# Gates and branch outputs of a decoder layer computed with tokens as the stationary operand

## The chip, the core and the metric

The kernel runs on one core of one Trainium2 chip. The metric is the device time of one execution in microseconds (us). TensorE (PE in the profile) multiplies: a stationary operand of 128x128 is loaded (LDWEIGHTS, the row PEld), a moving operand streams through it, and the products are summed in PSUM. VectorE (DVE), ScalarE (ACT) and GpSimd (POOL) do the rest, and SyncE (SP) issues nearly all DMAs.

## The reference

One layer, 256 tokens, 2048 features, all in float32. Three branches (convolution A, gated linear attention B, block attention C) work on the same normalised input `h`. The part that is changed is the merge of the branches:

```python
y_a = conformer_conv_branch(...)      # ends in  a @ w_conv_out[i]   (512 -> 2048)
y_b = gla_branch(...)                 # ends in  o @ w_gla_out[i]    (512 -> 2048)
y_c = moba_branch(...)                # ends in  o @ w_moba_out[i]   (1024 -> 2048)
gates = jax.nn.sigmoid(h @ w_gate[i] + b_gate[i]).reshape(b_sz, s, N_BRANCH, d)
merged = gates[:, :, 0] * y_a + gates[:, :, 1] * y_b + gates[:, :, 2] * y_c
x = x + merged @ w_out[i]
```

After it come a gated MLP with a short causal convolution and a gated input embedding, which the change leaves alone.

## The kernel before, in words

**Chunks.** Every weight matrix is read once, in chunks of 256 rows x 512 columns (512 KB). A chunk `c` goes through a ring of four buffers: SP loads it into `raw` (L323) once DVE has split the chunk four before it (`chunk_split`); ACT casts it to `w_hi` (`high`, L801), once PE has used chunk `c`-4 (`chunk_used`); DVE computes `w_lo = raw - w_hi` (`split`, L1084); PE multiplies. Each product is made of three matmuls, high by high, high by low and low by high, in the type fp32r.

**Two shapes of a chunk on PE.** `feature_chunk` (L457) holds a 128x128 block of the weights stationary and moves the 256 tokens of the activations: 2 x 4 blocks x 3 products = 24 matmuls of 256 columns. The result has features on partitions, as `[P, 4, 256]`. `token_chunk` (L481) holds 128 tokens x 128 features of the activations stationary and moves 512 weight columns: 2 halves of the tokens x 2 x 3 = 12 matmuls of 512 columns. The result has tokens on partitions, as `[P, 2, 512]`. Both fill the same two PSUM banks of an accumulator (`acc[0]` or `acc[1]`, by turns).

**Groups.** The program is a fixed list of 254 chunks, then loops for the MLP. A group of chunks makes 512 output columns. Around the change the list reads `mv` (chunks 74 to 89, two groups of 8), `yA` (90 to 97, four groups of 2), `gA` (98 to 129, four groups of 8), `yB` (130 to 137), `gB` (138 to 169), `yC` (170 to 185, four groups of 4), `gC` (186 to 217), `wout` (218 to 249, four groups of 8), `ple` (250 to 253). `y` are the branches' output projections, `g` the gates. `mv`, `wout` and `ple` use the token shape, the `y` and `g` groups the feature shape: 32 + 96 = 128 chunks. `LAST[name, g]` is the last chunk of a group.

**Order on the engines.** No scheduler is at work: each engine has a written program over `c`, and what hangs on a chunk number stands behind that chunk's own step. ACT's and DVE's steps for chunk `c` run when PE is some three chunks behind, because the cast of `c` waits until PE has used `c`-4. What an engine does beside its chunks is put at offsets: for the group `gC, g`, ACT computes `gt = tanh(0.5 a + 0.5 bias)` in four instructions (L905, one per 128 features, since the bias is one number per partition) behind the cast of `LAST`+4; DVE multiplies `yb = (gt + 1) yb` (L1389) and adds `full = merged + yb` (L1395) behind the split of `LAST`+5; ACT casts `full` to `m_hi` (L805) and DVE makes `m_lo` (L1090), which `wout` uses as the stationary operand, 128 tokens of 128 features. For `gA` and `gB` the multiplication stands at `LAST`+6. ACT copies the `y` groups out of PSUM (L850).

**Other work between the chunks.** In `yA` and `gA` PE also does the last levels of the linear attention (`gla_level`, behind chunks 91, 95, 99, 103, 107, each waiting for DVE's `level_ready`), its outputs and norms (112, 117, 119). From `yB` to the middle of `gB` it does eight attention heads, three small pieces each (`scores`, `turn_probs`, `probs_v`). Behind chunk 190 it turns `p`. In `wout` `turn_x` (L607) transposes 128x128 blocks of `x`, eight matmuls at a time. That makes 33 such pieces in chunks 90 to 217.

Of the kernel before, what the change touches and what calls it, by code (L numbers as in the profile page):

```python
# [37 lines left out]
P = 128  # L38
# [78 lines left out]
R_MIX, R_CB, R_LG, R_LB, R_GLA, R_Q, R_K, R_BG, R_FFN, R_PLE, R_ALL = 0, 16, 20, 24, 28, 29, 30, 31, 79, 95, 111  # L117
# [8 lines left out]
def trunk(nc, x, p, norm_mix_g, w_in, conv_w, conv_b, conv_ln_g, conv_ln_b, w_conv_out,  # L126
# [36 lines left out]
    small = new("small", [P, 16])  # L163
    arena = (top[0] + KB - 1) // KB * KB
# [17 lines left out]
    merged = ar("merged", [P, KD, S], 0)  # L182
    yb = ar("yb", [P, KD, S], 16)
# [15 lines left out]
    gt = ar("gt", [P, QD, S], 86)  # L199
# [62 lines left out]
    gate_ready, gate_merged = sem("gate_ready"), sem("gate_merged")  # L262
    p_turned = sem("p_turned")
# [30 lines left out]
    def wait_taken(eng, n):  # L294
# [12 lines left out]
            (gla_norm_g[0], R_GLA), (moba_q_norm_g[0], R_Q), (moba_k_norm_g[0], R_K), (b_gate[0], R_BG),  # L307
# [8 lines left out]
    def _(sp):  # L316
# [15 lines left out]
        for name, g, c0, n in GROUPS:  # L332
            if name == "gB" and g == 1:
                sp.wait_ge(chunk_used, FIRST["gB", 0])
                sp.dma_start(ptok[:], p[0, 0].rearrange("(t p) n -> p t n", p=P)).then_inc(p_landed, 16)
            for j in range(n):
# [113 lines left out]
    def _(pe):  # L450
# [166 lines left out]

        for c in range(UP1):
# [10 lines left out]
            if name in ("val", "gate", "qk", "gr", "mq", "mk", "mq2", "mk2", "gA", "gB", "gC"):  # L629
# [3 lines left out]
            elif name in ("gv", "mv"):  # L633
# [9 lines left out]
            elif name == "yA":  # L643
                pe.wait_ge(unit_split, U_A + 1)
                feature_chunk(c, s, a_hi, a_lo, 2 * j, first, last)
            elif name == "yB":
                pe.wait_ge(unit_split, U_B + 1)
                feature_chunk(c, s, o_hi, o_lo, 2 * j, first, last)
            elif name == "yC":
                pe.wait_ge(unit_split, U_C + 2 * j + 2)  # L650
                feature_chunk(c, s, c_hi, c_lo, 2 * j, first, last)
# [77 lines left out]
            for q in range(4):  # L729
                if c == LAST["wout", q] + 1:  # L730
                    turn_x(q, NUMBER["wout", q], U_X1 + q - 1 if q >= 2 else None)
# [49 lines left out]
    def _(act):  # L781
# [63 lines left out]

        def take(number, dst, src, scale=None):
# [5 lines left out]
        for c in range(START, UP1 + 12):  # L852
# [4 lines left out]
            if e in GROUP_AT and e == LAST[GROUP_AT[e][:2]] and not (GROUP_AT[e][0] == "ple" and e == c - RING):  # L857
# [30 lines left out]
                elif name == "yA":  # L888
                    take(number, merged[:, 4 * g:4 * g + 4, :], a[:], 0.5)
                elif name in ("yB", "yC"):  # L890
# [4 lines left out]
                    take(number, yb[:, 4 * g:4 * g + 4, :], a[:], 0.5)  # L895
                elif name in ("gA", "gB", "gC"):
                    b = "ABC".index(name[1])

                    if b == 2 and g:
                        act.wait_ge(unit_full, U_M + g)  # L900
                    elif 4 * b + g:
                        act.wait_ge(gate_merged, 4 * b + g)
                    for j in range(QD):
                        col = R_BG + 16 * b + 4 * g + j
# [658 lines left out]
```

## Time and profile before

| | |
|---|---|
| median of 3 runs | 1628.25 us (1627.68 to 1631.37) |
| the profiled execution | 1627.26 us, of which the span is 1625.3 us |
| granted TensorE clock, mean over the span | 0.998 of full speed |
| PE busy | 1609.0 us (99%) |
| DVE busy | 1031.2 us (63%) |
| ACT busy | 779.5 us (48%) |
| DMA | 294.30 MB, mean 181 GB/s |

The span is the time between the first and the last instruction; 2 us of the execution lie around it. Matmuls are pipelined, so a PE busy of 99% only says that there are no long holes; how fast it goes is read from the distance between the starts of its matmuls. A timeline row gives the start in us from the span's start, the duration in us, the engine, the line, the operation, the tiles written and read, and behind them in brackets how long the engine was idle before and what ended that.

### The profile page before, as it was taken

What the parts mean: (1) busy time and instruction counts of PE and PEld (TensorE: products, weight loads), DVE (VectorE), ACT (ScalarE), POOL (GpSimd) and SP (SyncE); (2) the same over time, 40 slices, a digit from 0 to 9 for tenths busy, and PEclk for the clock granted to TensorE, in tenths of its full rate; (3) what the DMA queues carried; (4) which work ended last, traced back from release to release, by engine and by line L of the source; (5) the groups of instructions that cost most, each with busy time, mean ns of one, the idle gap of its engine ahead of it and who ended that gap; (6) DMA issues with size and microseconds to landing.
All of it is one profiled execution on the core that took longest, in us unless ns stands there. A gap on an engine that the chain in (4) does not pass through costs nothing.

```text
span 1625.3 us, 26115 instructions
## 1 busy us (share of the span) xinstructions
PE 1609.0 (99%) x10146; PEld 1459.3 (90%) x10146; DVE 1031.2 (63%) x1203; ACT 779.5 (48%) x935; POOL 32.3 (2%) x53
## 2 busy tenths in 40 slices
PE   7999999999999999999999999999999999999998
PEld 7989998999999999988788888888888888888887
DVE  6598655664557545555467777765447777765554
ACT  5444444444455544455455555543335455554443
POOL 5000000000000000000000000000000000000000
PEclk9999999999999999999999999999999999999999
DMA  7666555555555565555566665655565666556564
GB/s 232 181 178 181 159 166 156 156 167 155 178 169 157 171 191 181 178 189 186 175 181 193 186 188 182 186 199 194 193 191 174 194 194 193 184 185 194 175 202 148
DMA packets 154275, 294.30 MB, mean 181 GB/s; under 512 B 9383, under 2 KB 11795, under 8 KB 154192
## 3 DMA queue, kind: packets, MB, share of 16 engines
q1 hardware_dynamic: 153648, 292.85, 58.6%
q8 instruction: 60, 0.98, 0.2%
q0 software_dynamic: 512, 0.27, 0.1%
q14 instruction: 23, 0.19, 0.0%
q10 hardware_dynamic: 32, 0.01, 0.0%
HBM read 291.00 MB, written 2.10 MB: 180 GB/s over the span
## 4 chain that ended last, share of the span: by engine, by line
PE 98%; DVE 1%; DMA 0%; ACT 0%; issue 0%; POOL 0%; SPq 0%; ACTq 0%; DVEq 0%
PE psum L474 20%; PE psum L453 12%; PE psum L454 11%; PE psum L455 11%; PE psum L477 10%; PE psum L490 10%; PE psum L491 10%; PE psum L492 10%; PE psum L570 1%; PE psum L507 1%; DMA xtok<-in_x 0%; PE psum L615 0%; PE psum L524 0%; PE psum L584 0%; PE psum L603 0%; PE psum L593 0%
## 5 line engine op out<-in xcount | busy, mean ns | idle before, releaser
L1084 DVE TENSOR_TENSOR w_lo<-raw,w_hi 128x1024 fp32r<-128x1024 f32 x550 | 670.1, 1223 | 518.1 <-ACT w_hi L801 517.8
L801 ACT CAST w_hi<-raw 128x1024 fp32r<-128x1024 f32 x550 | 574.8, 1049 | 666.8 <-PE psum L455 290.7
L453 PE MATMUL psum<-h_both,w_hi 128*128 128x256 f32 x1296 | 371.1, 286 | 3.0 <-DVE h_both L1090 3.0
L455 PE MATMUL psum<-h_both,w_lo 128*128 128x256 f32 x1296 | 367.6, 284 | 0.0
L454 PE MATMUL psum<-h_both,w_hi 128*128 128x256 f32 x1296 | 367.6, 284 | 0.0
L474 PE MATMUL psum<-h_both,w_hi 128*128 128x512 f32 x1408 | 352.6, 392 | 0.0
L474 PEld LDWEIGHTS psum<-h_both,w_hi 128*128 128x128 f32 x1408 | 253.3, 189 | 45.3
L453 PEld LDWEIGHTS psum<-h_both,w_hi 128*128 128x128 f32 x1296 | 249.6, 193 | 3.6 <-issue 3.2
L454 PEld LDWEIGHTS psum<-h_both,w_hi 128*128 128x128 f32 x1296 | 249.7, 193 | 0.1
L455 PEld LDWEIGHTS psum<-h_both,w_lo 128*128 128x128 f32 x1296 | 249.5, 192 | 0.0
L477 PEld LDWEIGHTS psum<-h_both,w_lo 128*128 128x128 f32 x1408 | 192.1, 190 | 13.7
L477 PE MATMUL psum<-h_both,w_lo 128*128 128x256 f32 x1408 | 196.3, 282 | 0.0
L490 PE MATMUL psum<-w_hi,f_hi 128*128 128x512 f32 x352 | 137.2, 390 | 0.0
L492 PE MATMUL psum<-w_hi,f_lo 128*128 128x512 f32 x352 | 137.0, 389 | 0.0
L491 PE MATMUL psum<-w_lo,f_hi 128*128 128x512 f32 x352 | 137.0, 389 | 0.0
L490 PE MATMUL psum<-w_hi,h_both 128*128 128x512 f32 x224 | 87.8, 392 | 0.0
L491 PE MATMUL psum<-w_lo,h_both 128*128 128x512 f32 x224 | 87.2, 389 | 0.0
L492 PE MATMUL psum<-w_hi,h_both 128*128 128x512 f32 x224 | 87.2, 389 | 0.0
L492 PEld LDWEIGHTS psum<-w_hi,f_lo 128*128 128x128 f32 x352 | 66.1, 188 | 13.8
L490 PEld LDWEIGHTS psum<-w_hi,f_hi 128*128 128x128 f32 x352 | 66.1, 188 | 13.6
L491 PEld LDWEIGHTS psum<-w_lo,f_hi 128*128 128x128 f32 x352 | 66.1, 188 | 13.4
L1169 DVE SCALAR_TENSOR_TENSOR val<-apad,cw,val 128x256 f32<-128x256 f32 x120 | 50.2, 480 | 1.1
(248 smaller groups left out, 1466.7 us busy)
## 6 DMA issues: line engine op xcount, KB each, us to landing
raw<-in_w_up SPq DMA_DIRECT2D x176, 512.0 KB, 3.8
raw<-in_w_gate SPq DMA_DIRECT2D x96, 512.0 KB, 3.7
raw<-in_w_in SPq DMA_DIRECT2D x90, 512.0 KB, 3.6
raw<-in_w_down SPq DMA_DIRECT2D x88, 512.0 KB, 4.5
raw<-in_w_out SPq DMA_DIRECT2D x32, 512.0 KB, 4.4
raw<-in_w_ple_gate SPq DMA_DIRECT2D x32, 512.0 KB, 4.5
raw<-in_w_moba_out SPq DMA_DIRECT2D x16, 512.0 KB, 3.7
raw<-in_w_conv_out SPq DMA_DIRECT2D x8, 512.0 KB, 3.7
```

The source lines that it names most:

```text
L453: nc.tensor.matmul(dst, stat_hi, mov_hi, start=first, stop=False, skip_group_check=True)
L454: nc.tensor.matmul(dst, stat_hi, mov_lo, start=False, stop=False, skip_group_check=True)
L455: return nc.tensor.matmul(dst, stat_lo, mov_hi, start=False, stop=last, skip_group_check=True)
L474: nc.tensor.matmul(wide[part][:, j, :], w_hi[:, c % RING, w], h_both[:, kt + k, :, :].rearrange("p h s -> p (h s)"), start=first and k == ...
L477: mm = nc.tensor.matmul(wide[part][:, j, S:2 * S], w_lo[:, c % RING, w], h_hi[:, kt + k, :], start=False, stop=last and k == 1, skip_group ...
L490: nc.tensor.matmul(o, sh, w_hi[:, c % RING, w], start=first and k == 0, stop=False, skip_group_check=True)
L491: nc.tensor.matmul(o, sh, w_lo[:, c % RING, w], start=False, stop=False, skip_group_check=True)
L492: mm = nc.tensor.matmul(o, sl, w_hi[:, c % RING, w], start=False, stop=last and k == 1, skip_group_check=True)
L507: mm = nc.tensor.matmul(dst[:, 2 * j + t:2 * j + t + 1], src[:, j, t * P:(t + 1) * P], ones[:, 0:1], start=True, stop=True, skip_group_che ...
L801: A.copy(w_hi[:, c % RING, :], raw[:, c % RING, :]).then_inc(chunk_high, 1)
L1084: V.tensor_tensor(w_lo[:, c % RING, :], raw[:, c % RING, :], w_hi[:, c % RING, :].bitcast(F32), ALU.subtract).then_inc(chunk_split, 1)
L1169: last = V.scalar_tensor_tensor(val[:, j, :], src, w, val[:, j, :], ALU.mult, ALU.add)
```

## The change

The `y` and `g` groups use the token shape. Their results, `merged`, `yb` and `gt` lie with tokens on partitions. Since the gate's bias then differs along the row, it is no longer a number per partition: SP loads 512 of its values ahead of each `g` group, repeated on all 128 partitions (256 KB in SBUF, twelve times), DVE adds it to the sums out of PSUM (`gate_sum`, behind the split of `LAST`+3), and ACT computes one `tanh` of 128x1024 in place. The multiplication of `gC` moves to `LAST`+4. The merged result has tokens on partitions, while `wout` needs features there, so PE turns it by eight transposes per group (`turn_m`, behind chunk `LAST`+2 of `gC`), and ACT and DVE make `m_hi` and `m_lo` out of PSUM (`m_high` at `LAST`+6, `m_low` at `LAST`+7). ACT's waits on `gate_merged` ahead of the gates are gone. The rows of the bias leave the small parameters' table, which falls from 111 rows to 63.

```diff
     rows = [(norm_mix_g[0], R_MIX), (conv_b[0], R_CB), (conv_ln_g[0], R_LG), (conv_ln_b[0], R_LB),
-            (gla_norm_g[0], R_GLA), (moba_q_norm_g[0], R_Q), (moba_k_norm_g[0], R_K), (b_gate[0], R_BG),
+            (gla_norm_g[0], R_GLA), (moba_q_norm_g[0], R_Q), (moba_k_norm_g[0], R_K),
             (norm_ffn_g[0], R_FFN), (norm_ple_g[0], R_PLE)]
...
                 sp.dma_start(ptok[:], p[0, 0].rearrange("(t p) n -> p t n", p=P)).then_inc(p_landed, 16)
+            if name in ("gA", "gB", "gC"):
+                k = 4 * "ABC".index(name[1]) + g
+                if k >= 2:
+                    wait_taken(sp, NUMBER["g" + "ABC"[(k - 2) // 4], (k - 2) % 4])
+                sp.dma_start(bias[:, k % 2, :], b_gate[0, k * W:(k + 1) * W].unsqueeze(0).broadcast_to([P, W])).then_inc(bias_landed[k % 2], 16)
             for j in range(n):
...
 
+        def turn_m(g):
+
+            pe.wait_ge(unit_full, U_M + g + 1)
+            if g >= 2:
+                pe.wait_ge(unit_split, U_M + g - 1)
+            src = tokens(full[:, (U_M + g) % 2, :, :])
+            for j in range(QD):
+                for t in range(TT):
+                    mm = nc.tensor.transpose(turned(g)[:, j, t * P:(t + 1) * P], src[:, t, j * P:(j + 1) * P], ident[:])
+            mm.then_inc(m_turned, 1)
+
         for c in range(UP1):
...
             first, last = j == 0, j == n - 1
-            if name in ("val", "gate", "qk", "gr", "mq", "mk", "mq2", "mk2", "gA", "gB", "gC"):
+            if name in ("val", "gate", "qk", "gr", "mq", "mk", "mq2", "mk2"):
                 if c < START:
                     pe.wait_ge(unit_split, U_H + c + 1)
                 feature_chunk(c, s, h_hi, h_lo, 2 * j, first, last)
-            elif name in ("gv", "mv"):
+            elif name in ("gv", "mv", "gA", "gB", "gC"):
                 token_chunk(c, s, h_hi, h_lo, 2 * j, first, last)
...
                 pe.wait_ge(unit_split, U_A + 1)
-                feature_chunk(c, s, a_hi, a_lo, 2 * j, first, last)
+                token_chunk(c, s, a_hi, a_lo, 2 * j, first, last)
             elif name == "yB":
                 pe.wait_ge(unit_split, U_B + 1)
-                feature_chunk(c, s, o_hi, o_lo, 2 * j, first, last)
+                token_chunk(c, s, o_hi, o_lo, 2 * j, first, last)
             elif name == "yC":
                 pe.wait_ge(unit_split, U_C + 2 * j + 2)
-                feature_chunk(c, s, c_hi, c_lo, 2 * j, first, last)
+                token_chunk(c, s, c_hi, c_lo, 2 * j, first, last)
             elif name == "wout":
...
             for q in range(4):
+                if c == LAST["gC", q] + 2:
+                    turn_m(q)
                 if c == LAST["wout", q] + 1:
...
 
+        def m_high(g):
+
+            act.wait_ge(m_turned, g + 1)
+            A.copy(m_hi[:, QD * g:QD * g + QD, :], turned(g)).then_inc(unit_high, 1)
+
         def take(number, dst, src, scale=None):
...
                 elif name == "yA":
-                    take(number, merged[:, 4 * g:4 * g + 4, :], a[:], 0.5)
+                    take(number, merged[:, :, g * W:(g + 1) * W], tokens(a), 0.5)
                 elif name in ("yB", "yC"):
                     if name == "yB" and g == 0:
                         act.wait_ge(att_ready, 1)
                     if name == "yC":
                         act.wait_ge(gate_merged, 4 + g + 1)
-                    take(number, yb[:, 4 * g:4 * g + 4, :], a[:], 0.5)
+                    take(number, yb[:, :, g * W:(g + 1) * W], tokens(a), 0.5)
                 elif name in ("gA", "gB", "gC"):
-                    b = "ABC".index(name[1])
-
-                    if b == 2 and g:
-                        act.wait_ge(unit_full, U_M + g)
-                    elif 4 * b + g:
-                        act.wait_ge(gate_merged, 4 * b + g)
-                    for j in range(QD):
-                        col = R_BG + 16 * b + 4 * g + j
-                        last = A.activation(gt[:, j, :], a[:, j, :], ACT.Tanh, bias=parh[:, col:col + 1], scale=0.5)
-                    last.then_inc(taken[number % 2], 1)
+                    wait_taken(act, number)
+                    A.activation(gt[:], gt[:], ACT.Tanh, scale=0.5).then_inc(gate_ready, 1)
                 elif name == "ple":
...
             for g in range(4):
-                if c == LAST["gC", g] + 5:
+                if c == LAST["gC", g] + 6:
                     earlier()
-                    unit(U_M + g)
+                    m_high(g)
                 if c == LAST["wout", g] + 4:
...
 
+        def gate_sum(k, last_chunk, number):
+
+            dve.wait_ge(chunk_used, last_chunk + 1)
+            dve.wait_ge(bias_landed[k % 2], 16 * (k // 2 + 1))
+            V.tensor_tensor(gt[:], tokens(acc[number % 2]), bias[:, k % 2, :].unsqueeze(1).broadcast_to([P, TT, W]),
+                            ALU.add).then_inc(taken[number % 2], 1)
+
+        def m_low(g):
+
+            dve.wait_ge(unit_high, U_M + g + 1)
+            m = slice(QD * g, QD * g + QD)
+            V.tensor_tensor(m_lo[:, m, :], turned(g), m_hi[:, m, :].bitcast(F32), ALU.subtract).then_inc(unit_split, 1)
+
         def x_mean(n):
...
                     name = "g" + "ABC"[b]
-                    q = slice(4 * g, 4 * g + 4)
-                    if c == LAST[name, g] + (6 if b < 2 else 5):
+                    q = slice(g * W, (g + 1) * W)
+                    if c == LAST[name, g] + 3:
                         earlier()
-                        wait_taken(dve, NUMBER[name, g])
+                        gate_sum(4 * b + g, LAST[name, g], NUMBER[name, g])
+                    if c == LAST[name, g] + (6 if b < 2 else 4):
+                        earlier()
+                        dve.wait_ge(gate_ready, 4 * b + g + 1)
+                        wait_taken(dve, NUMBER["y" + "ABC"[b], g])
                         if b == 0:
-                            wait_taken(dve, NUMBER["yA", g])
-                            V.scalar_tensor_tensor(merged[:, q, :], gt[:], 1.0, merged[:, q, :], ALU.add, ALU.mult).then_inc(gate_merged, 1)
+                            V.scalar_tensor_tensor(merged[:, :, q], gt[:], 1.0, merged[:, :, q], ALU.add, ALU.mult).then_inc(gate_merged, 1)
                         else:
-                            wait_taken(dve, NUMBER["yB" if b == 1 else "yC", g])
-                            step(V.scalar_tensor_tensor(yb[:, q, :], gt[:], 1.0, yb[:, q, :], ALU.add, ALU.mult))
+                            step(V.scalar_tensor_tensor(yb[:, :, q], gt[:], 1.0, yb[:, :, q], ALU.add, ALU.mult))
                             sync()
                             if b == 1:
-                                V.tensor_tensor(merged[:, q, :], merged[:, q, :], yb[:, q, :], ALU.add).then_inc(gate_merged, 1)
+                                V.tensor_tensor(merged[:, :, q], merged[:, :, q], yb[:, :, q], ALU.add).then_inc(gate_merged, 1)
                             else:
 
-                                V.tensor_tensor(full[:, (U_M + g) % 2, :, :], merged[:, q, :], yb[:, q, :], ALU.add).then_inc(unit_full, 1)
-                    if b == 2 and c == LAST[name, g] + 6:
+                                V.tensor_tensor(tokens(full[:, (U_M + g) % 2, :, :]), merged[:, :, q], yb[:, :, q],
+                                                ALU.add).then_inc(unit_full, 1)
+                    if b == 2 and c == LAST[name, g] + 7:
                         earlier()
-                        unit(U_M + g)
+                        m_low(g)
             if c == FIRST["gC", 0] + 8:
```

How the order moves is shown at two places, both in the gates of branch C. First PE, from the end of the last chunk but one ahead of the turn into the chunk behind it, with the change (`w_hi` and `w_lo` are the chunk's halves, `h_both` the normalised input, `full` the merged group, `ident` the unit matrix):

```order
L498 MATMUL psum<-w_hi,h_both 128x512
L499 MATMUL psum<-w_lo,h_both 128x512
L500 MATMUL psum<-w_hi,h_both 128x512
L634 MATMUL psum<-ident,full 128x128 x8
L498 MATMUL psum<-w_hi,h_both 128x512
L499 MATMUL psum<-w_lo,h_both 128x512
```

The same place before, where nothing stands between the chunks:

```order
L453 MATMUL psum<-h_both,w_hi 128x256
L454 MATMUL psum<-h_both,w_hi 128x256
L455 MATMUL psum<-h_both,w_lo 128x256
L453 MATMUL psum<-h_both,w_hi 128x256
L454 MATMUL psum<-h_both,w_hi 128x256
```

The matmuls are half as many and twice as wide, and eight transposes stand between two chunks.

Then DVE, in the group `gC, 0` and up to the next group's gate; before (`p_lo` is the low part of the embedding input, which has its place here too):

```order
L1402 COPY full<-psum 128x512
L1084 TENSOR_TENSOR w_lo<-raw,w_hi 128x1024 x2
L1090 TENSOR_TENSOR p_lo<-full,p_hi 128x512
L1084 TENSOR_TENSOR w_lo<-raw,w_hi 128x1024 x2
L1389 SCALAR_TENSOR_TENSOR yb<-gt,yb 128x1024
L1395 TENSOR_TENSOR full<-merged,yb 128x1024
L1084 TENSOR_TENSOR w_lo<-raw,w_hi 128x1024
L1090 TENSOR_TENSOR m_lo<-full,m_hi 128x1024
L1084 TENSOR_TENSOR w_lo<-raw,w_hi 128x1024 x7
```

and with the change (`bias` is the repeated bias):

```order
L1436 COPY full<-psum 128x512
L1102 TENSOR_TENSOR w_lo<-raw,w_hi 128x1024 x2
L1169 TENSOR_TENSOR gt<-psum,bias 128x1024
L1108 TENSOR_TENSOR p_lo<-full,p_hi 128x512
L1102 TENSOR_TENSOR w_lo<-raw,w_hi 128x1024
L1422 SCALAR_TENSOR_TENSOR yb<-gt,yb 128x2x512
L1428 TENSOR_TENSOR full<-merged,yb 128x1024
L1102 TENSOR_TENSOR w_lo<-raw,w_hi 128x1024 x3
L1176 TENSOR_TENSOR m_lo<-psum,m_hi 128x1024
L1102 TENSOR_TENSOR w_lo<-raw,w_hi 128x1024 x4
```

The addition of the bias is new, the multiplication stands one split earlier, and `m_lo` two splits further behind the merge.

## Rows read from the trace of the kernel before

**Rows 1.** The page: busy times, and the chain that ended last.
```profile
PE 1609.0 (99%) x10146; PEld 1459.3 (90%) x10146; DVE 1031.2 (63%) x1203; ACT 779.5 (48%) x935; POOL 32.3 (2%) x53
...
PE 98%; DVE 1%; DMA 0%; ACT 0%; issue 0%; POOL 0%; SPq 0%; ACTq 0%; DVEq 0%
```

**Rows 2.** Waits of PE: what for, us in total, times, longest.
```profile
PE psum L534 <- DMA pst<-in_norm_mix_g: 3.9, 1, 3.9
PE psum L524 <- POOL ms L396: 3.1, 2, 2.3
PE psum L453 <- DVE h_both L1090: 3.0, 1, 3.0
PE psum L544 <- DMA xtok<-in_x: 1.0, 1, 1.0
```

**Rows 3.** Windows: length, busy time and count by engine, clock, DMA.
```profile
624.58:647.62 23.04, 23.04 (x195) 23.04 (x193) 13.70 (x12) 10.80 (x13) 0.00 (x0) 1.00 0.58 183
427.00:555.00 128.00, 128.00 (x1049) 127.11 (x1048) 79.43 (x119) 68.72 (x108) 0.00 (x0) 1.00 0.55 167
248.23:259.11 10.88, 10.88 (x49) 9.01 (x48) 4.85 (x7) 5.23 (x6) 0.00 (x0) 1.00 0.68 190
```

**Rows 4.** Timeline of PE in `wout`: a turn of `x` between token matmuls.
```profile
717.98 0.39 PE L492 MATMUL psum<-w_hi,m_lo 128*128 128x512 f32 x1
718.21 1.03 PE L615 MATMUL psum<-ident,xtok 128*128 128x128 f32 x8
719.00 0.48 PE L490 MATMUL psum<-w_hi,m_hi 128*128 128x512 f32 x1
719.32 0.40 PE L491 MATMUL psum<-w_lo,m_hi 128*128 128x512 f32 x1
```

**Rows 5.** Timeline of PE in `gA`: sixteen small matmuls between feature matmuls.
```profile
396.21 0.28 PE L455 MATMUL psum<-h_both,w_lo 128*128 128x256 f32 x1
396.33 1.95 PE L524 MATMUL psum<-ident,ms 128*128 128x128 f32 x16
398.03 0.36 PE L453 MATMUL psum<-h_both,w_hi 128*128 128x256 f32 x1
...
398.59 0.28 PE L454 MATMUL psum<-h_both,w_hi 128*128 128x256 f32 x1
```

**Rows 6.** Timeline of PE in `mv`: the same sixteen between token matmuls.
```profile
270.49 0.39 PE L492 MATMUL psum<-w_hi,h_both 128*128 128x512 f32 x1
...
272.41 0.48 PE L490 MATMUL psum<-w_hi,h_both 128*128 128x512 f32 x1
...
273.43 0.39 PE L491 MATMUL psum<-w_lo,h_both 128*128 128x512 f32 x1
```

**Rows 7.** Timeline of ACT at the end of the group `gC, 1` (chunk 201).
```profile
647.87 1.05 ACT L801 CAST w_hi<-raw 128x1024 fp32r<-128x1024 f32 x1 [1.83 <-PE psum L455]
648.95 1.57 ACT L905 ACTIVATE gt<-psum,parh 128x256 f32<-128x256 f32 x4
650.75 1.05 ACT L801 CAST w_hi<-raw 128x1024 fp32r<-128x1024 f32 x1 [0.23 <-PE psum L455]
```

**Rows 8.** Groups by shape, chunks 90 to 217: busy, mean ns, idle before.
```profile
L1389 DVE SCALAR_TENSOR_TENSOR yb<-gt,yb 128x1024 f32<-128x1024 f32 x7 | 8.6, 1225 | 0.2
L850 ACT ACTIVATE yb<-psum 128x1024 f32<-128x1024 f32 x8 | 8.2, 1025 | 0.3
...
L1342 DVE TENSOR_TENSOR full<-gr,psum 128x1024 f32<-128x1024 f32 x1 | 1.2, 1223 | 0.0
...
L1090 DVE TENSOR_TENSOR p_lo<-full,p_hi 128x512 fp32r<-128x512 f32 x1 | 0.7, 691 | 0.0
```

**Rows 9.** Timeline of DVE: the merge of `gC, 1`.
```profile
654.35 1.23 DVE L1395 TENSOR_TENSOR full<-merged,yb 128x1024 f32<-128x1024 f32 x1
```

**Rows 10.** Timeline of DVE: what the last attention level waits for.
```profile
355.21 0.68 DVE L1206 TENSOR_TENSOR lqk<-gqk,ex 128x512 f32<-128x512 f32 x1
```

**Rows 11.** Timeline of PE: that level, behind chunk 107.
```profile
356.63 0.72 PE L573 MATMUL psum<-lqk 64*128 64x128 f32 x8
```

**Rows 12.** Timeline of SP: the load of chunk 206 is the first of these.
```profile
641.56 20.14 SPq L323 DMA_DIRECT2D raw<-in_w_gate  x7
```

**Rows 13.** DMA issues by line: KB each, median us to landing.
```profile
raw<-in_w_gate SPq DMA_DIRECT2D x96, 512.0 KB, 3.7
...
ptok<-in_p SPq DMA_DIRECT2D x1, 256.0 KB, 4.3
```

More of the change, by code:

```diff
@@ L114 @@
 U_X2 = U_F + PAIRS1 + PAIRS2
-R_MIX, R_CB, R_LG, R_LB, R_GLA, R_Q, R_K, R_BG, R_FFN, R_PLE, R_ALL = 0, 16, 20, 24, 28, 29, 30, 31, 79, 95, 111
+R_MIX, R_CB, R_LG, R_LB, R_GLA, R_Q, R_K, R_FFN, R_PLE, R_ALL = 0, 16, 20, 24, 28, 29, 30, 31, 47, 63
 START = 8
@@ L163, in trunk @@
     small = new("small", [P, 16])
+    bias = new("bias", [P, 2, W])
     arena = (top[0] + KB - 1) // KB * KB
@@ L181, in trunk @@
     masks = ar("masks", [P, 7, P // 2], 28)
-    merged = ar("merged", [P, KD, S], 0)
-    yb = ar("yb", [P, KD, S], 16)
+    merged = ar("merged", [P, TT, D], 0)
+    yb = ar("yb", [P, TT, D], 16)
     mq = ar("mq", [P, HEADS, S], 32)
@@ L198, in trunk @@
     tmpg = ar("tmpg", [P, QD * S], 82)
-    gt = ar("gt", [P, QD, S], 86)
+    gt = ar("gt", [P, TT, W], 86)
     o_hi = ar("o_hi", [P, QD, S], 68, F32R)
@@ L262, in trunk @@
     gate_ready, gate_merged = sem("gate_ready"), sem("gate_merged")
+    bias_landed = [sem("bias_landed0"), sem("bias_landed1")]
+    m_turned = sem("m_turned")
     p_turned = sem("p_turned")
```

## The prediction

> **What bounds the kernel now.** I read the page's busy times and the chain that ended last first [rows 1]: PE is busy for 99% of the span, and 98% of the last chain lies on PE. Such a share says nothing of how fast PE goes, so the list of PE's waits came next [rows 2]. It has four rows, 11.0 us together, and all of them belong to the start, before or at the first chunks. From then on PE waits for nobody: neither for a split, nor for the attention pieces, nor for a load. So the time of the stage that is changed is the distance between the starts of PE's matmuls, and only what changes that distance, or makes PE wait, moves the end.
>
> The windows give the distance for both shapes [rows 3]. The group `gC, 1` is 8 feature chunks of 24 matmuls, 192 in 23.04 us: 0.120 us each and 2.88 us a chunk. (The count 195 holds three more that reach over the window's edges.) Four token chunks in `mv`, 48 matmuls, take 10.88 us: 0.2267 us each and 2.72 us a chunk. The granted clock is 1.00 in both. The token shape moves the same columns in half as many instructions, and it is 0.16 us a chunk faster, on the same input `h` as the gates use.
>
> **What the shape gives.** 128 chunks (32 of `y`, 96 of `g`) x 0.16 us = 20.5 us, all of it on PE and therefore on the path.
>
> Here the Trainium skill speaks against the change. Its page "TensorE: Matmul & The Clock Gate", section "Back-to-back issue gap", gives an isolated matmul 262 cycles for 256 columns and 518 for 512, almost the columns alone. By that, 24 narrow matmuls and 12 wide ones would differ by 72 cycles or 0.03 us, and the 128 chunks would give 3.8 us. The trace disagrees with it for a stream of weight load and matmul: 0.120 us and 0.2267 us are both above its 0.109 and 0.216 us, and the narrow one by more in proportion.
>
> **What PE gets in addition.** (a) Four turns of the merged result, eight 128x128 transposes each. `wout` shows such a turn between token chunks [rows 4]: from 717.98 to 719.32 us lie two steps between the chunks' own matmuls, which take 0.45 us undisturbed, so the turn costs 0.89 us. Four cost 3.6 us. (b) The 33 small pieces between chunks 90 and 217 now stand beside token chunks. The same sixteen small matmuls cost 2.38 - 5 x 0.12 = 1.78 us between feature matmuls [rows 5] and 2.94 - 5 x 0.2267 = 1.81 us between token matmuls [rows 6]. 33 x 0.03 = 1.0 us; I keep 0 and 1.5 us as its ends, since only one kind of piece is seen in both surroundings.
>
> **Waits that could come.** Let T be the moment at which PE starts the chunk behind a gate's group; for `gC, 1` it is 647.62 us [rows 3]. The cast that waits for the same semaphore starts at T+0.25 [rows 7]. The new addition of the bias can start there too; it is an elementwise operation of 128x1024 with one operand in PSUM, 1.22 us [rows 8] (L1342), and ends at T+1.5. The tanh in one instruction I price as ACT's 128x1024 out of PSUM, 1.03 us [rows 8] (L850); it ends at T+2.55. DVE's split of `LAST`+4 goes from T+1.5 to T+2.7, the multiplication to T+3.95, the addition to T+5.2 (1.225 us each [rows 8, 9]). PE comes to the turn two chunks on, at T+5.44, but fetches the weights of a matmul one step earlier, so it looks at about T+5.2. That is a tie: 0 to 0.3 us of waiting, and I take 0.1 us for three of the turns. In the first group DVE also has the low part of the embedding input in between, 0.69 us [rows 8] (L1090): the merge is ready at T+5.9, and I take 0.6 us. Together 0.9 us. As the other end I take the moment at which the merge is ready today, 655.58 us or T+7.96 [rows 9]: if the earlier place in the order gained nothing, each turn would wait 2.5 us, 10 us in all.
>
> The chain of the attention levels has the least air of the other waits. For the last level DVE ends at 355.21 + 0.68 = 355.89 us [rows 10], and PE starts it at 356.63 [rows 11]. DVE's part hangs on the end of chunk 105, and the three chunks from there to the level get 3 x 0.16 = 0.48 us shorter, so 0.26 us of 0.74 are left, less PE's look ahead. The new bias addition of `gA, 0` stands in that very stretch of DVE, but DVE is idle there while ACT makes the exponentials. I take 0.1 us, between 0 and 0.5.
>
> **What lies beside.** The bias additions, 12 x 1.22 = 14.7 us of DVE, cost nothing in themselves: DVE is busy 13.70 of 23.04 us in `gC, 1` and 79.43 of 128 us in the densest stretch of attention heads [rows 3], with 14.9 of 22.7 us and some 84 of 123 us afterwards. Behind each addition stand a split and the merge, and PE needs that split three chunks later. ACT loses four small tanh (1.57 us, [rows 7]) for one of 1.03 us, and its cast no longer stands behind a wait for the merge. `m_high` and `m_low` are as long as the instructions that they replace; the last of them is done by about T+12 us, and `wout` asks for it at its seventh chunk, T+17. Where that cover went, PE would wait for the difference once. The one bias DMA of POOL that goes is at the start, off the path.
>
> The twelve repeated loads stand in SP's queue ahead of a group's first chunk, and everything behind them waits for them. SP's own wait ahead of them is for an addition eight chunks or more ago, done by then. How much they may take: the load of chunk 206 is issued at 641.56 us [rows 12], lands 3.7 us later [rows 13], and its cast starts at 650.75 [rows 7], a margin of 5.5 us, and of 4.8 us with four chunks 0.16 us shorter. A plain load of the same 256 KB lands in 4.3 us [rows 13], and it shares the engines rather than holding them. I take 0, with the case below as the other end.
>
> **The sum.** 20.5 - 3.6 - 1.0 - 0.9 - 0.1 = 14.9 us. The profiled execution takes 1627.26 us, so 1612.4 us; the median of the runs is 1.0 us above the profiled one, and I predict 1613.4 us. With nothing waiting and the pieces no dearer the gain is 16.9 us; with every turn waiting 2.5 us it is 5 to 6 us.
>
> **Rivals.**
> 1. *The turns wait as long as the merge takes today.* Each link of addition, tanh, split, multiplication and addition passes a semaphore, and the tie at T+5.2 bears no extra. Full price 4 x 2.6 = 10.4 us in place of 0.9, gain 5.4, time 1622.9 us. Against it: the merge moves forward by a whole split, and each link's duration is known. Chance 0.13, with most of that for a part of the price.
> 2. *The levels and heads come late.* PE's time between two of them shrinks by 0.16 us a chunk and DVE has the additions in between. Eight heads at 0.5 us are 4 us: 1617.4 us. For it speaks the 0.26 us of the last level; against it that no head shows a wait now [rows 2]. Chance 0.05.
> 3. *Only columns count.* Then the shape gives nothing, and the turns, pieces and waits remain, 5.6 us: 1633.9 us. With the 3.8 us it is 1630.1 us, no measurable change (that part of the case is the skill's rule on the issue gap). Four chunks at 2.72 us against eight at 2.88 us [rows 3] speak plainly against it. Chance 0.02.
> 4. *Slower: the repeated load holds the queue.* All 128 partitions read the same 2 KB. If such a transfer were confined to one of the 16 DMA engines, it would go at 183 / 0.58 / 16 = 20 GB/s [rows 3] and take 13 us; the chunk behind it would be 8.5 us late, twelve times 102 us, time about 1715 us. It decides from 4.8 + 14.9 / 12 = 6.0 us per load on; above that the kernel is slower than before. The only 256 KB load in the trace, 4.3 us, is below, but repeats nothing. Chance 0.03.
>
> **How the numbers follow.** The forecast has 0.77. Its own spread is 1611 to 1616 us. The range, 1610.8 to 1618 us, takes in the case with no waits and dearer or cheaper pieces, the second rival and the small part of the first; outside lie its full price and the last two. A measurement of this kernel tells about 0.2% or 3.3 us from no change. The forecast and the first two rivals are faster, 0.95; the third, near no change, 0.02; the fourth slower, 0.03.
>
> **What the profile of the changed kernel would show.** A group of `gC` between turns in 21.8 us, 0.227 us from matmul to matmul; four transposes of `full` by eight, the first with a wait for DVE of about half a microsecond, the others with none or 0.1 us; no other new wait of PE; bias loads that land in 3 to 5 us; the stages behind `ple` as long as before and some 15 us earlier. I would be wrong if a token chunk in the `y` or `g` groups took more than 2.75 us, if the turns showed waits of 1 us and more each, or if casts of ACT stood waiting for `raw`.

## The result, and the profile after

| | before | changed |
|---|---|---|
| median | 1627.97 us (1626.97 to 1631.37, 4 runs) | 1613.89 us (1611.17 to 1614.10, 4 runs) |
| profiled execution, span | 1627.26 us, 1625.3 us | 1614.08 us, 1612.0 us |

The ratio is 0.9906 with a 95% interval of 0.9888 to 0.9924: the change takes 14.1 us off, where 14.9 us and a time of 1613.4 us were predicted. A later set of runs of both kernels gave 1611.92 us against 1628.60 us, 16.7 us off.

The page of the changed kernel, answering to [rows 1]:

```profile
PE 1596.1 (99%) x8642; PEld 1383.0 (86%) x8642; DVE 1044.7 (65%) x1215; ACT 774.5 (48%) x899; POOL 32.3 (2%) x52
...
PE 97%; DVE 1%; DMA 1%; ACT 1%; issue 0%; POOL 0%; SPq 0%; DVEq 0%; ACTq 0%
```

PE has 1504 matmuls fewer (128 chunks x 12, less 4 x 8 transposes) and is still the bound. Its waits, answering to [rows 2]:

```profile
PE psum L542 <- DMA pst<-in_norm_mix_g: 4.3, 1, 4.3
PE psum L461 <- DVE h_both L1108: 3.0, 1, 3.0
PE psum L532 <- POOL ms L404: 2.3, 1, 2.3
PE psum L552 <- DMA xtok<-in_x: 0.7, 1, 0.7
PE psum L498 <- DVE w_lo L1102: 0.4, 1, 0.4
PE psum L634 <- DVE full L1428: 0.2, 1, 0.2
```

Four are old. One of these, `ms` L404, is 2.3 us long and stands between `ple` and the MLP, in both kernels; it matters below. Of the two new waits, L634 is the first turn. L498 is at the very end, where DVE's split stands in its queue behind a wait for an output DMA to land; nothing of the change is near it.

Windows of the changed kernel, with the columns of [rows 3]: eight chunks of `yC`, and the stretch around the start of the MLP.

```profile
565.10:586.86 21.76, 21.76 (x98) 18.02 (x97) 9.81 (x8) 10.44 (x10) 0.00 (x0) 1.00 0.65 211
778.00:800.00 22.00, 19.74 (x101) 16.83 (x100) 10.46 (x16) 9.34 (x10) 1.60 (x1) 0.92 0.54 161
```

The first shows 96 matmuls in 21.76 us, 2.72 us a chunk, as read from `mv` ahead of the change. The DMAs now bring 211 GB/s and nobody waits for them. The second has a granted clock of 0.92, of which more below.

The trace can be cut at the first matmul of every chunk, since the order on PE is fixed. The next table gives the time between such starts in us for each stage; it was worked out from the two traces and is no view of the profile:

| stretch | before | changed | difference |
|---|---|---|---|
| up to the first chunk | 16.43 | 15.43 | -1.00 |
| chunks 0 to 89 (unchanged groups) | 281.39 | 282.03 | +0.64 |
| `yA` | 26.47 | 25.31 | -1.16 |
| `gA` | 102.61 | 97.77 | -4.84 |
| `yB` | 25.23 | 24.06 | -1.17 |
| `gB` | 102.90 | 98.74 | -4.16 |
| `yC` | 46.08 | 43.52 | -2.56 |
| `gC` (three turns) | 92.59 | 90.65 | -1.94 |
| `wout` (one turn), `ple` | 98.87 | 99.68 | +0.81 |
| from the last `ple` chunk to the end | 832.70 | 834.83 | +2.13 |

From `yA` to `ple` the sum is -15.0 us: 20.5 us from the shape, less 4.0 us for the turns and 1.5 us for the 33 small pieces. The last line is no part of the change: 1.5 us is a lower clock at the start of the MLP, and 0.6 us lies at the very end, around the wait for the output's DMA. In the first two lines PE starts 1.0 us earlier, but more of the low clock at the start (6.8 us long in both traces) then falls into chunks 0 and 1, which gives 0.4 us back (together -0.6 us); 0.25 us more is spent at chunk 10.

The turn in `gC`, in the timeline of PE of the changed kernel:

```profile
637.39 0.39 PE L500 MATMUL psum<-w_hi,h_both 128*128 128x512 f32 x1
637.62 1.03 PE L634 MATMUL psum<-ident,full 128*128 128x128 f32 x8
638.41 0.48 PE L498 MATMUL psum<-w_hi,h_both 128*128 128x512 f32 x1
638.72 0.39 PE L499 MATMUL psum<-w_lo,h_both 128*128 128x512 f32 x1
```

Read as [rows 4]: 638.72 - 637.39 - 2 x 0.2267 = 0.88 us, and no wait in brackets. DVE's side of it, with T = 632.18 us:

```profile
632.43 1.22 DVE L1169 TENSOR_TENSOR gt<-psum,bias 128x1024 f32<-128x1024 f32 x1 [0.41 <-PE psum L500]
633.57 1.22 DVE L1102 TENSOR_TENSOR w_lo<-raw,w_hi 128x1024 fp32r<-128x1024 f32 x1
634.90 1.23 DVE L1422 SCALAR_TENSOR_TENSOR yb<-gt,yb 128x1024 f32<-128x1024 f32 x1
636.16 1.23 DVE L1428 TENSOR_TENSOR full<-merged,yb 128x1024 f32<-128x1024 f32 x1
```

The merge ends at 637.39 us, T+5.21, and PE starts the first weight load of the turn at 637.44 us, T+5.26. The tie that the prediction saw is there, and it comes out with nothing lost. The first group has `p_lo` in between, and there the turn waits:

```profile
614.32 0.39 PE L500 MATMUL psum<-w_hi,h_both 128*128 128x512 f32 x1
614.89 1.09 PE L634 MATMUL psum<-ident,full 128*128 128x128 f32 x8 [0.18 <-DVE full L1428]
615.74 0.48 PE L498 MATMUL psum<-w_hi,h_both 128*128 128x512 f32 x1
```

The bracket says 0.18 us, but the start is 0.57 us behind the last chunk matmul in place of 0.23. The weight load waits for the merge too: here it starts at 614.89 us, together with its matmul, where in the other turn it started 0.18 us ahead of it. The wait costs 0.4 us in chunk starts (3.91 us for this chunk against 3.51 us for the three others).

### The profile page after: what moved, and what is told of

It is laid out like the page before. It is cut to its first block, busy times and chain, and to the rows that moved or that the text cites. A ratio compares the mean times of both kernels' runs of the same rounds, so it can differ in the third digit from the quotient of the medians.

```text
span 1612.0 us, 23109 instructions
## 1 busy us (share of the span) xinstructions
PE 1596.1 (99%) x8642; PEld 1383.0 (86%) x8642; DVE 1044.7 (65%) x1215; ACT 774.5 (48%) x899; POOL 32.3 (2%) x52
## 4 chain that ended last, share of the span: by engine, by line
PE 97%; DVE 1%; DMA 1%; ACT 1%; issue 0%; POOL 0%; SPq 0%; DVEq 0%; ACTq 0%
PE psum L482 20%; PE psum L498 17%; PE psum L500 17%; PE psum L499 17%; PE psum L485 10%; PE psum L461 4%; PE psum L462 4%; PE psum L463 4%; PE psum L578 1%; PE psum L515 1%; PE psum L623 0%; PE psum L532 0%; DMA out<-fin 0%; DVE w_lo L1102 0%; ACT junk L839 0%; DMA xtok<-in_x 0%
## 5 line engine op out<-in xcount | busy, mean ns | idle before, releaser
L482 PEld LDWEIGHTS psum<-h_both,w_hi 128*128 128x128 f32 x1408 | 254.2, 190 | 45.6
L498 PE MATMUL psum<-w_hi,h_both 128*128 128x512 f32 x608 | 240.5, 396 | 0.4 <-DVE w_lo L1102 0.4
L500 PE MATMUL psum<-w_hi,h_both 128*128 128x512 f32 x608 | 236.9, 390 | 0.0
L499 PE MATMUL psum<-w_lo,h_both 128*128 128x512 f32 x608 | 236.8, 389 | 0.0
L485 PEld LDWEIGHTS psum<-h_both,w_lo 128*128 128x128 f32 x1408 | 192.1, 190 | 13.7
L485 PE MATMUL psum<-h_both,w_lo 128*128 128x256 f32 x1408 | 196.3, 282 | 0.0
L461 PE MATMUL psum<-h_both,w_hi 128*128 128x256 f32 x528 | 151.6, 287 | 3.0 <-DVE h_both L1108 3.0
L462 PE MATMUL psum<-h_both,w_hi 128*128 128x256 f32 x528 | 150.5, 285 | 0.0
L463 PE MATMUL psum<-h_both,w_lo 128*128 128x256 f32 x528 | 150.5, 285 | 0.0
L498 PE MATMUL psum<-w_hi,f_hi 128*128 128x512 f32 x352 | 137.2, 390 | 0.0
L500 PEld LDWEIGHTS psum<-w_hi,h_both 128*128 128x128 f32 x608 | 114.1, 188 | 24.4
L498 PEld LDWEIGHTS psum<-w_hi,h_both 128*128 128x128 f32 x608 | 114.2, 188 | 24.1 <-DVE w_lo L1102 0.8
L499 PEld LDWEIGHTS psum<-w_lo,h_both 128*128 128x128 f32 x608 | 114.3, 188 | 22.5
L461 PEld LDWEIGHTS psum<-h_both,w_hi 128*128 128x128 f32 x528 | 102.5, 194 | 3.4 <-issue 3.2
L462 PEld LDWEIGHTS psum<-h_both,w_hi 128*128 128x128 f32 x528 | 102.6, 194 | 0.1
L463 PEld LDWEIGHTS psum<-h_both,w_lo 128*128 128x128 f32 x528 | 102.5, 194 | 0.0
```

The lines of the kernel that those rows point to most:

```text
L461: nc.tensor.matmul(dst, stat_hi, mov_hi, start=first, stop=False, skip_group_check=True)
L462: nc.tensor.matmul(dst, stat_hi, mov_lo, start=False, stop=False, skip_group_check=True)
L463: return nc.tensor.matmul(dst, stat_lo, mov_hi, start=False, stop=last, skip_group_check=True)
L482: nc.tensor.matmul(wide[part][:, j, :], w_hi[:, c % RING, w], h_both[:, kt + k, :, :].rearrange("p h s -> p (h s)"), start=first and k == ...
L485: mm = nc.tensor.matmul(wide[part][:, j, S:2 * S], w_lo[:, c % RING, w], h_hi[:, kt + k, :], start=False, stop=last and k == 1, skip_group ...
L498: nc.tensor.matmul(o, sh, w_hi[:, c % RING, w], start=first and k == 0, stop=False, skip_group_check=True)
```

## The experiments

**Two narrow matmuls in place of a wide one.** In the gate chunks, same operands, same layout, same everything around:

```diff
-nc.tensor.matmul(o, sh, w_hi[:, c % RING, w], ...)          # 512 columns, three products
+parts = 2 if narrow else 1                                   # narrow: gA, gB, gC
+n_ = W // parts
+for q_ in range(parts):
+    o = dst[:, t * W + q_ * n_:t * W + (q_ + 1) * n_]
+    w = slice(k * W + q_ * n_, k * W + (q_ + 1) * n_)
+    nc.tensor.matmul(o, sh, w_hi[:, c % RING, w], ...)       # and the two other products
```

> The changed kernel, but in the 96 gate chunks each product of 512 columns is issued as two of 256 with the same stationary operand, so a chunk is again 24 matmuls of 256 columns while layout, bias, tanh and turns stay as changed. Theory: the gain is a fixed cost per matmul, 0.2267 us = 512/2.4 GHz + 13 ns and 0.120 us = 256/2.4 GHz + 13 ns, so 12 matmuls less are 0.16 us. Expected 0.120 us from start to start and 2.88 us a chunk in the gates, 96 x 0.16 = 15.4 us longer than the changed kernel, about 1629 us. Rival: the gain comes from what is stationary (128 tokens of h against weight blocks that were just written, or the repeat of the same stationary operand); then a chunk stays near 2.72 us and the time near 1614 us.

Measured 1628.63 us (10 runs), 0.9994 of the kernel before (0.9984 to 1.0004). `gA` takes 102.60 us and `gB` 102.90 us, to a hundredth what they took before the change. Four of its gate chunks in a window:

```profile
409.20:420.72 11.52, 11.52 (x98) 11.52 (x97) 6.12 (x5) 4.19 (x4) 0.00 (x0) 1.00 0.57 183
```

96 matmuls in 11.52 us, 0.120 us each. The rival falls: neither what is held stationary nor the layout matters, only into how many instructions the columns are cut. Bias loads, added bias and new tanh are all still there, so the run also shows that they cost the stages `gA` and `gB` nothing.

**Four of 128 columns.** The same with `parts = 4`.

> As the previous one, with four pieces of 128 columns: 48 matmuls a gate chunk. If the cost is columns/2.4 GHz + 13 ns at every width, one takes 0.067 us and a chunk 3.2 us, the kernel 96 x 0.48 = 46 us above the changed one, about 1660 us. Rival: below some width the weight load between two matmuls sets the pace (the small attention matmuls of 64 columns start 0.10 us apart); then a matmul takes about 0.10 us, a chunk 4.8 us, and the kernel is some 200 us above, about 1814 us.

Measured 1920.19 us (one run). Two windows of it, the first at a granted clock of 1.00, the second at 0.50:

```profile
528.02:549.46 21.44, 21.44 (x194) 21.44 (x194) 6.13 (x5) 4.19 (x4) 0.00 (x0) 1.00 0.32 100
380.00:440.00 60.00, 60.00 (x285) 59.66 (x284) 10.33 (x10) 6.28 (x6) 0.00 (x0) 0.50 0.19 57
```

At 2.4 GHz, 192 matmuls take 21.44 us, 0.112 us each: hardly less than one of 256 columns. So columns/2.4 GHz + 13 ns (0.120 - 0.107 and 0.2267 - 0.2133 us) holds for 256 and 512 columns and not for 128, where a pair of weight load and matmul takes 0.112 us in place of 0.067. That is the rival's case. Its 48 x 0.112 = 5.36 us a chunk give 253 us, and the kernel is 306 us above the changed one; the rest is the second row. PE was issuing without a hole, and the clock stood at 1.2 GHz for 95.6 us of `gA` and, 31 us later, for 20.5 us more of it; at 0.21 us a matmul in place of 0.112 that is some 54 us. The same stream in `gB` and `gC` kept 2.4 GHz. No expectation had the fall, and why it came in `gA` alone is open.

At 1.2 GHz the fixed cost is gone. A matmul of 512 columns takes 0.427 us there (the run below), exactly 512/1.2 GHz, and one of 256 takes 0.213 us, exactly 256/1.2 GHz, as in the first chunk of the kernel before:

```profile
18.49 0.41 PE L453 MATMUL psum<-h_both,w_hi 128*128 128x256 f32 x1
18.70 0.41 PE L454 MATMUL psum<-h_both,w_hi 128*128 128x256 f32 x1
18.91 0.41 PE L455 MATMUL psum<-h_both,w_lo 128*128 128x256 f32 x1
```

One of 128 columns takes 0.21 us as well (285 in 60.00 us). So the gain of the wide shape exists at the full clock only, and the floor of narrow pieces doubles when the clock is halved.

**The merge one split later.**

```diff
-if c == LAST[name, g] + (6 if b < 2 else 4):
+if c == LAST[name, g] + (6 if b < 2 else 5):
```

> The changed kernel with the multiplication of branch C's gates one split later on DVE (behind LAST+5, where it stood before the change), the turns left where they are. Theory: the early place in the order is what keeps the four turns from waiting. The merge is then ready 7.8 us after the chunk behind the group starts, PE looks at 5.2 us: a wait of about 2.6 us at each turn in place of 0.4 us at the first, 10 us in all, about 1624 us (the first rival of the prediction at its full price). If waits of this length also let the granted TensorE clock fall, each costs up to 1.7 us more, and the time goes to 1631 us. If DVE's order didn't matter it would stay at 1614 us.

Measured 1625.96 us (10 runs), 12.1 us above the changed kernel. The turns' row in PE's list of waits, and the second turn:

```profile
PE psum L634 <- DVE full L1428: 9.0, 4, 2.3
```

```profile
640.38 0.39 PE L500 MATMUL psum<-w_hi,h_both 128*128 128x512 f32 x1
643.02 1.38 PE L634 MATMUL psum<-ident,full 128*128 128x128 f32 x8 [2.25 <-DVE full L1428]
644.05 0.78 PE L498 MATMUL psum<-w_hi,h_both 128*128 128x512 f32 x1
644.62 0.63 PE L499 MATMUL psum<-w_lo,h_both 128*128 128x512 f32 x1
645.05 0.63 PE L500 MATMUL psum<-w_hi,h_both 128*128 128x512 f32 x1
```

The turn starts 2.64 us after the last chunk matmul in place of 0.23 us, and its chunk takes 2.5 to 2.7 us more than without a wait (2.1 us more at the first, which waited before), 9.7 us in all. Behind two of the four the matmuls stand 0.43 us apart, 1.2 GHz; the two chunks with this stretch take 4.27 and 4.41 us against 2.83 us, 3.0 us together. Both parts of the expectation came true, the clock after two waits of four. So the prediction's first rival was a real danger with about the price that it named (10.4 us), and what keeps it away is one place in DVE's order.

**One transpose in place of eight.** `for j in range(1): for t in range(1)` in `turn_m`, so seven of a group's eight blocks are left unturned, and the result is not the layer's.

> The changed kernel with one of the eight transposes in each of the four turns, so most of the merged result isn't turned. If a turn costs its eight transposes of about 0.1 us each and a restart of the chunk stream of 0.1 us, then 7 x 0.1 = 0.7 us go at each turn: 2.8 us less in the windows of the turns. The first turn's wait for DVE, 0.4 us, stays. Rival: the turns cost by their place (the stream of 512-column matmuls is broken); then nearly all of the 0.9 us stays.

Measured 1608.21 us (one run). A turn now reads:

```profile
635.75 0.39 PE L500 MATMUL psum<-w_hi,h_both 128*128 128x512 f32 x1
635.98 0.27 PE L634 MATMUL psum<-ident,full 128*128 128x128 f32 x1
636.01 0.47 PE L498 MATMUL psum<-w_hi,h_both 128*128 128x512 f32 x1
636.32 0.40 PE L499 MATMUL psum<-w_lo,h_both 128*128 128x512 f32 x1
```

The two chunks around it take 2.75 and 2.82 us, 0.13 us above 2 x 2.72, against 0.91 us with eight. Seven transposes are 0.78 us, 0.11 us each, and the broken stream costs 0.1 us. `gC` and the stage behind it are 2.3 and 0.7 us shorter, 3.0 us in all for the 2.8 us expected. The whole span is 5.7 us below that of the changed kernel. Of the 2.7 us left over, 1.8 us lie behind `ple`, where the clock did not fall in this execution, and 0.9 us in front of `yA`, where the low stretch at the start lasted 3.4 us in place of 6.8.

**The gap ahead of the MLP.** The changed kernel's profile has this, where PE waits for GpSimd's square root:

```profile
779.68 0.39 PE L500 MATMUL psum<-w_hi,p_lo 128*128 128x512 f32 x1
782.33 1.19 PE L532 MATMUL psum<-ident,ms 128*128 128x128 f32 x4 [2.26 <-POOL ms L404]
783.17 3.25 PE L482 MATMUL psum<-h_both,w_hi 128*128 128x512 f32 x8
```

Eight matmuls in 3.25 us, against 2.0 us otherwise: most of them ran at 1.2 GHz, 0.43 us apart. The profile of the kernel before has the same wait, and its clock stayed. One experiment fills the wait, before `spread(8, fb_flat, 1)`:

```diff
+for _ in range(9):
+    nc.tensor.matmul(fa[:, 0, :], m_hi[:, 0, 0:P], m_hi[:, 0:2, :].rearrange("p k s -> p (k s)"), start=True, stop=True, ...)
```

> The changed kernel with nine matmuls of 512 columns, whose result is not used, put on PE ahead of the spread that waits for GpSimd's square root between the embedding product and the MLP. In the changed kernel's profile PE stands 2.3 us there, the granted clock then reads 1.2 GHz for 3.4 us, and the same stretch is 1.5 us longer than in the kernel before, which has the same wait and kept 2.4 GHz. Theory: the clock fell because PE stood, and filling the wait (2.0 us of it) keeps the clock up: no low stretch there, 1.5 us less than in the executions of the changed kernel that had it, and the median 1 to 1.5 us below the changed kernel. Rival: the low stretch comes with the changed position of the work in time alone, whatever PE does; then it stays and the time is the same, or 0.3 us more where the filler delays the spread.

Measured 1612.35 us (4 runs). Its profile:

```profile
779.15 2.20 PE L755 MATMUL psum<-m_hi 128*128 128x512 f32 x9
781.47 0.71 PE L532 MATMUL psum<-ident,ms 128*128 128x128 f32 x4
781.94 2.10 PE L482 MATMUL psum<-h_both,w_hi 128*128 128x512 f32 x8
```

No low stretch, and the part from the last `ple` chunk to the end takes 832.56 us against 834.83. One profile can't tell this from chance, but there are eleven traces. Nine have the wait unfilled; the clock fell behind it in seven and stayed in two (the kernel before and the one with one transpose). Two have it filled, this run and the next, and it fell in neither. If the filler did nothing, that would still happen about once in twenty times (2/9 x 2/9, an estimate). So the theory is likely and not shown. The median is no help: the changed kernel, run again beside this one, had 1611.92 us, so the 1 to 1.5 us that were expected don't show in whole times.

**Three small edits together**, that filler, the table of 111 rows, and `unit(U_P)` on DVE at `FIRST["gC", 0] + 12` in place of `+ 10`:

> The changed kernel with three small edits: the filler matmuls of the previous run, the table of small parameters with the gate's bias rows again (111 rows in place of 63, so that its transposes hold more than 64 rows), and the low part of the embedding input on DVE two chunks later, behind the merge of the first gate group of C. Expected by stage: the 2.3 us wait filled and no low clock there (1.5 us), the five table transposes back from 0.55 to 0.39 us plus restart (0.25 us), the first turn as cheap as the others (0.4 us): 2.2 us below the changed kernel, about 1611.8 us. If only the waits named go and the clock falls anyhow, 0.65 us.

Measured 1611.14 us (6 runs, 1610.38 to 1618.11), ratio to the kernel before 0.9903 (0.9888 to 0.9918). By stage everything expected is there: the part behind `ple` has no low stretch, the first turn's chunk takes 3.51 us in place of 3.91, chunk 10 takes 3.27 in place of 3.52, the last part 832.9 in place of 834.8.

**The changed kernel again**, beside the last two:

> The changed kernel once more, as the comparison for the others of this chip: 1613.9 us as before. If the 3.4 us of low clock behind the embedding product is a matter of chance from execution to execution, the profile may show it or not, with 1.5 us of difference in the stage behind.

Measured 1611.92 us (4 runs, 1611.07 to 1613.67), ratio 0.9894 (0.9880 to 0.9908). That is 2.0 us less than the 1613.9 us expected; its profile shows the low stretch behind `ple` again. So as a whole time the version with three edits can't be told from the changed kernel; its 0.65 us without the clock are smaller than the spread of the executions. That spread goes with the clock: of the changed kernel's eight executions, the spans of 1611.7 to 1612.1 us have a mean granted clock of 0.997 and those of 1609.0 to 1610.8 us have 0.998. The longest execution of the version with three edits, a span of 1616.0 us, has 0.994 although its gap is filled, so the clock also falls elsewhere. Two traces show one such place, where PE waits for nothing: behind the 32 small matmuls that follow chunk 79. This is the run with the late merge; the bias run below has the same, and the other nine traces do not:

```profile
260.72 1.84 PE L515 MATMUL psum<-ones,sqm 128*128 128x1 f32 x16
262.49 1.61 PE L578 MATMUL psum<-lqk 64*128 64x64 f32 x16
...
264.82 0.62 PE L498 MATMUL psum<-w_hi,h_both 128*128 128x512 f32 x1
265.25 0.63 PE L499 MATMUL psum<-w_lo,h_both 128*128 128x512 f32 x1
```

Chunk 80 then takes 4.45 us in place of 2.85.

**The table of small parameters.**

```diff
-R_MIX, R_CB, R_LG, R_LB, R_GLA, R_Q, R_K, R_FFN, R_PLE, R_ALL = 0, 16, 20, 24, 28, 29, 30, 31, 47, 63
+R_MIX, R_CB, R_LG, R_LB, R_GLA, R_Q, R_K, R_BG, R_FFN, R_PLE, R_ALL = 0, 16, 20, 24, 28, 29, 30, 31, 79, 95, 111
```

> The changed kernel with the small parameters' table of 111 rows as before the change. In the changed kernel chunk 10 with its five transposes takes 3.515 us against 3.269 us before, although the first transpose shrank from 111 to 63 rows. Theory: a stationary operand of 64 rows or fewer can't be fetched while a matmul over all rows runs, as at the attention levels' 64-row operands, whose first matmul starts 0.21 us behind the last chunk matmul in place of 0.12; with 111 rows chunk 10 takes 3.27 us again. Rival: the difference comes from elsewhere (when the table's DMAs land), and chunk 10 stays at 3.5 us.

Measured 1613.24 us (one run); chunk 10 takes 3.267 us, and took 3.269 us before the change. The changed kernel first, then this one:

```profile
49.54 0.28 PE L463 MATMUL psum<-h_both,w_lo 128*128 128x256 f32 x1
49.75 0.76 PE L682 MATMUL psum<-ident,pst 63*128 63x63 f32 x5
50.30 0.36 PE L461 MATMUL psum<-h_both,w_hi 128*128 128x256 f32 x1
```

```profile
49.63 0.28 PE L463 MATMUL psum<-h_both,w_lo 128*128 128x256 f32 x1
49.75 0.60 PE L682 MATMUL psum<-ident,pst 111*128 111x111 f32 x5
50.13 0.36 PE L461 MATMUL psum<-h_both,w_hi 128*128 128x256 f32 x1
```

The smaller first transpose starts 0.21 us behind the chunk in place of 0.12 us, and the five together take longer. The size of the table is the cause. The rows of the weight loads show what is late: with 111 rows the first load starts at 49.65 us, 0.10 us ahead of its matmul, and with 63 rows at 49.75 us, together with it. That the border lies at 64 rows was not tried.

**Ten of the twelve bias loads left out.** The other ten groups add the first two groups' values again, and DVE no longer waits for the loads that are gone.

```diff
+if k < 2:
     sp.dma_start(bias[:, k % 2, :], b_gate[0, k * W:(k + 1) * W]...)
...
-dve.wait_ge(bias_landed[k % 2], 16 * (k // 2 + 1))
+dve.wait_ge(bias_landed[k % 2], 16)
```

> The changed kernel with the repeated bias loaded for the first two gate groups only; the other ten groups add these values again, so their gates are not the reference's. Theory (the loads are hidden): they land in 3.9 us, inside the 4.8 us of margin of the chunk behind them, no cast of ACT waits for a load, and every stage from yA to wout is as long as in the changed kernel within 0.1 us. Rival (the prediction's slower case in a small measure): the loads hold up the chunks behind them a little; then gB and gC, with four loads each, get shorter by up to 0.5 us each.

Measured 1614.49 us (one run). `yA` to `ple` take 25.31, 97.77, 24.06, 98.74, 43.52, 90.65 and 99.68 us, in each stage the same hundredth as the changed kernel. The loads are wholly hidden, and the prediction's slower rival has nothing left, not even in small.

## Why the prediction was right

- *The bound.* Right: PE alone, before and after. One reading of [rows 2] was wrong: the four waits do not all belong to the start. The 2.3 us for POOL's `ms` stand at 795 us, between `ple` and the MLP, so PE does wait once behind the changed stage. The sum held no term for it and needed none, since both kernels have it; but the clock fell behind it in the changed kernel's profile.
- *The shape, 20.5 us.* Right in size: `yC`, which has nothing else in it, lost 2.56 us on 16 chunks, 0.160 us each. The reason is a fixed cost per matmul at the full clock, shown by the pieces of 256 columns. The third rival is dead. The Trainium skill's figures for an isolated matmul that were weighed (TensorE: Matmul & The Clock Gate, "Back-to-back issue gap": 262 and 518 cycles) would by an estimate have given 0.03 us a chunk; five times more was measured, so for this stream of fp32r pairs the trace was the better source.
- *The turns, 3.6 us and 0.9 us of waits.* Measured 1.31 us for the first and 0.91 us for each other, 4.0 us in all. The cost of a turn was right (0.9), the waits were too dear: 0.4 us for 0.6 us at the first, none for 0.1 us each at the others.
- *The pieces, 1.0 us.* Measured 1.5 us, 0.046 us a piece. The 0.03 us came from one kind of piece over the first few matmuls behind it. Chunk by chunk, most of it lies in the chunk behind a piece, 0.02 to 0.07 us; a part of that tail lay outside the rows read.
- *The attention levels, 0.1 us.* No level waits. The last one's chunk takes 3.46 us, as its width asks.
- *What lies beside.* Right, and tested: bias additions, tanh and loads cost nothing in the stages of the gates. The loads land in 3.7 to 5.3 us (median 3.9), under the 6.0 us from which they would have decided.
- *What was missing.* Four things that the sum had at nothing: the transposes of the smaller table (+0.25 us), the start and the end (-0.6 us and +0.6 us, neither by the change as far as the runs show), and a clock that fell once behind a wait of 2.3 us (1.5 us). Together they turn the 15.0 us of the stages into the 13.2 us between the two profiled executions; the clock is most of that. It was not the mechanism of a rival.
- *What was luck.* The 14.9 us met the 15.0 us of the stages so closely because two errors cancel: the waits were 0.5 us too dear and the pieces 0.5 us too cheap. The median was met by 0.5 us because two more do. The prediction put the median 1.0 us above the profiled execution, and it came out 0.2 us below; the profiled execution itself took 1.7 us more than the predicted 1612.4 us, mostly the clock's fall. The second set of runs, with 1611.92 us, is 1.5 us off on the other side. The mechanism and its size are right; half a microsecond of agreement is not evidence for them, the stages are.

## What to carry to other kernels

Where PE is the bound and every product is a pair of weight load and matmul, count the instructions: at 2.4 GHz each cost a fixed 13 ns here on top of its columns, so 512 columns a piece took 6% less than 256, whichever operand moves. Pieces of 128 columns were no quicker than 0.112 us each, 86% more time for the same work than with 256, and the clock fell as well. Turning a result by eight transposes costs 0.9 us if the data is there when PE looks. Whether it is was decided by one position in another engine's order, worth 12 us here. Compare stages between traces, not totals: a change of 0.25 us is plain in a chunk and invisible in a median that the clock moves by 3 us.

## What the runs showed of the hardware

- A stream of 128-column pairs ran at 0.112 us each, and with PE issuing all the time the granted clock was at 1.2 GHz for 95.6 us, then for 20.5 us, both in `gA`; in `gB` and `gC` it was not. The same work cut in 256 columns, and in 512 in the changed kernel, kept 2.4 GHz throughout the gates.
- The 13 ns beyond the columns appeared at 2.4 GHz only: 0.120 us for 256 columns and 0.2267 us for 512, against 0.213 and 0.427 us at 1.2 GHz. A pair of 128 columns took 0.112 and 0.21 us.
- Waits of PE of 2.3 us were followed by 3.4 us at 1.2 GHz in some cases and not in others: behind two of four in the kernel with the late merge, and ahead of the MLP in seven of nine traces. In two of eleven traces such a stretch came behind 32 small matmuls without any wait. Each one cost 1.4 to 1.6 us on top of the wait, if there was one.
- Five transposes took 0.16 us longer with a first operand of 63 rows than with one of 111.
